# Gate and up tiles of four feed-forward blocks as a two by two product of quarters, with seven quarter products in place of eight

## What is computed

```python
def rms_norm(x, gain):
    xf = x.astype(jnp.float32)
    y = xf * lax.rsqrt(jnp.mean(xf * xf, axis=-1, keepdims=True) + NORM_EPS)
    return (y * gain.astype(jnp.float32)).astype(x.dtype)
...
def modulate(x, shift, scale):
    return x * (1 + scale) + shift
...
def swiglu(h, w_gu, w_down):
    gate, up = jnp.split(h @ w_gu, 2, axis=-1)
    return (jax.nn.silu(gate) * up) @ w_down
```

## Time and profile before

| | us |
|---|---|
| median of 3 runs | 3361.91 (3359.94 to 3364.61) |
| profiled execution | 3367.02, its span 3365.3 |
| PE busy (matmul) | 3231.2, 96% of the span |
| DVE busy | 1817.0, 54% |
| ACT busy | 1157.8, 34% |
| POOL busy | 439.7, 13% |

### The profile page before, as it was taken

One profiled execution on the slowest core, in us unless ns is written; L12 is line 12 of the kernel. 1 busy time (PEld: TensorE's weight loads), 2 busy tenths in 40 slices (PEclk: granted clock), 3 DMA queues, 4 the chain that ended last, 5 costly groups with the idle time before them and its releaser, 6 DMA issues. The chain is left out here.

```text
span 3365.3 us, 67083 instructions
## 1 busy us (share of the span) xinstructions
PE 3231.2 (96%) x28066; PEld 2765.1 (82%) x28066; DVE 1817.0 (54%) x2677; ACT 1157.8 (34%) x1839; POOL 439.7 (13%) x312
## 2 busy tenths in 40 slices
PE   6999999999988999999999999999999989899998
PEld 5888888886667878888888888888886668789897
DVE  4552554565667655543554553454555766655353
ACT  3331222225665333321222431222224654344231
POOL 2000001000705310000002000001100616120000
PEclk9999999999999999999999999999999999999999
DMA  5231221342000012222221222222232000122222
GB/s 201 91 109 66 94 96 60 127 156 89 1 17 3 4 57 81 93 98 77 90 90 57 94 98 71 81 93 85 85 141 110 2 18 3 34 88 94 90 91 94
DMA packets 68270, 263.34 MB, mean 78 GB/s; under 512 B 7552, under 2 KB 8704, under 8 KB 67456
## 3 DMA queue, kind: packets, MB, share of 16 engines
q1 hardware_dynamic: 67664, 256.95, 22.1%
q10 hardware_dynamic: 432, 3.88, 0.3%
HBM read 258.70 MB, written 2.10 MB: 77 GB/s over the span
## 5 line engine op out<-in xcount | busy, mean ns | idle before, releaser
L240 PE MATMUL ps<-hn_hi,w_hi 128*128 128x512 f32 (+1 forms) x3520 | 864.8, 327 | 17.9 <-DVE hn_lo L457 5.9
L240 PE MATMUL ps<-hn_hi,w_lo 128*128 128x512 f32 (+1 forms) x3520 | 865.4, 327 | 0.0
L240 PE MATMUL ps<-hn_lo,w_hi 128*128 128x512 f32 (+1 forms) x3520 | 861.1, 326 | 0.0
L217 ACT ACTIVATE w_hi<-raw 128x1024 fp32r<-128x1024 f32 (+1 forms) x300 | 338.5, 1128 | 1375.4 <-PE ps L240 1217.7
L222 DVE TENSOR_TENSOR w_lo<-raw,w_hi 128x1024 fp32r<-128x1024 f32 (+1 forms) x300 | 396.9, 1323 | 469.5 <-ACT w_hi L217 462.0
L240 PEld LDWEIGHTS ps<-hn_hi,w_hi 128*128 128x128 f32 x3520 | 547.9, 190 | 82.3 <-issue 17.6
L240 PEld LDWEIGHTS ps<-hn_lo,w_hi 128*128 128x128 f32 x3520 | 548.3, 190 | 58.3
L240 PEld LDWEIGHTS ps<-hn_hi,w_lo 128*128 128x128 f32 x3520 | 545.2, 190 | 58.1
L240 PE MATMUL ps<-g_hi,w_hi 128*128 128x512 f32 (+1 forms) x1424 | 398.0, 347 | 6.1 <-DVE g_lo L894 6.1
L240 PE MATMUL ps<-g_lo,w_hi 128*128 128x512 f32 (+1 forms) x1424 | 403.5, 351 | 0.0
L240 PE MATMUL ps<-g_hi,w_lo 128*128 128x512 f32 (+1 forms) x1424 | 397.5, 347 | 0.0
(11 more groups left out here) (274 smaller groups left out, 3795.8 us busy)
## 6 DMA issues: line engine op xcount, KB each, us to landing
raw<-wgu SPq DMA_DIRECT2D x176, 512.0 KB, 3.4
w_mod_one<-wmod SPq DMA_DIRECT2D x100, 512.0 KB, 3.3
raw<-wdn SPq DMA_DIRECT2D x64, 704.0 KB, 4.1
raw<-win SPq DMA_DIRECT2D x44, 512.0 KB, 4.5
w_mod_two<-wmod SPq DMA_DIRECT2D x28, 512.0 KB, 3.6
w_mod_first<-wmod_first SPq DMA_DIRECT2D x4, 2048.0 KB, 23.2
raw<-wout SPq DMA_DIRECT2D x16, 512.0 KB, 3.3
h<-xT ACTq DMA_DIRECT2D x1, 3072.0 KB, 9.8
```

The lines of the kernel that those rows point to most:

```text
L217: act.activation(w_hi[s][:, 0:kt, :].rearrange("p k n -> p (k n)"), raw[s][:, 0:kt * P], ACT.Copy).then_inc(hi_ready[s].sem, 1)
L240: mm = pe.matmul(out[:, o:o + b - a], w[:, k, :], m[:, k, a:b], start=(k == 0 and w is w_hi[s] and m is mov_hi), stop=(k == kt - 1 and w i ...
```

## The change

Gate and up tile of one pair, and the two halves of the tokens, are seen as a matrix product of 2x2 blocks: the weights are split in four quarters (gate and up, first four and last four k-tiles, each 4 k-tiles x 128 = 512 columns of `raw0` or `raw1`), the moving operand in four quarters (first and second half of the tokens, first and last four k-tiles, each 4 tiles of 384+2 columns, or 256+2 for 512 tokens). Eight quarter products would give the four result blocks; here seven do, over sums and differences of quarters. The seven moving operands are made once for a block (`m_hi0..6`, `m_lo0..6`), the weight sums (`slot_sum2..5`) for each pair by POOL, and the products are combined out of PSUM by DVE (`combine`, seven additions of 384 or 386 columns for each pair) after a first copy by ACT (`first_copy`).

Since sums over the two token halves need like factors, the tokens are normalised first: `x_norm` = `gained_h` * `rstd`, before any product of the block. The in-between stages before a block leave `gained_h` in one fp32 copy and no longer split it.

The down product is made after groups of 4, 2, 4, 4, 4 and 4 pairs (`DOWN_SIZES`) rather than after 11 and 11, so there are six down stages of 8 tiles in a block. The operand of the down product is a ring of four tiles. `raw` holds 1024 columns. The modulation rows (24, as before) are placed in the groups 0, 2 and 3 and the down stages that follow them. The loops of `ffn` are written out.

The core of the diff:

```diff
-        WS = NFH * P * 4
+        WS = KD * P * 4 + 1568
...
+        def gained_plain(act, tile, nt):
+            for span, w in tokens_of(nt):
+                mm = act.activation(gained_h[:, bass.ds(tile, 1), span].rearrange("p a t -> p (a t)"),
+                                    h[:, bass.ds(tile, 1), span].rearrange("p a t -> p (a t)"), ACT.Identity,
+                                    scale=moda[:, w, bass.ds(tile, 1)])
+            mm.then_inc(hn_hi_ready.sem, 1)
...
+                    for j, z in enumerate(SIZES):
+                        for n in range(FIRST[j], FIRST[j] + z):
+                            load_mods(n)
+                            gate_raw_free(n)
+                            load(0, A["wdn"][l, which, j, 0] if last_of(n) else A["wgu"][l, which, 2 * n + 2])
+                            up_raw_free(n)
...
+                    rstd_of = lambda half: rstd_s[:, half * HT:(half + 1) * HT].rearrange("p (a t) -> p a t", a=1).broadcast_to([P, LP, HT])
+                    pool.wait_ge(hn_hi_ready.sem, hn_hi_ready.at(KD + 1))
+                    for half in range(2):
+                        pool.wait_ge(rstd_ready.sem, rstd_ready.at(half + 1))
+                        pool.tensor_tensor(x_norm[:, half, LP:KD, 0:HT], gained_h[:, LP:KD, half * HT:(half + 1) * HT],
+                                           rstd_of(half), ALU.mult).then_inc(x_pool.sem, 1)
+                    slot_lo_made(pool, 4, 0)
+                    slot_lo_made(pool, 3, 0)
+                    moving_lo(3, lambda k: m_raw[3][:, k, 0:HW], 13, "T4b")
+                    slot_lo_made(pool, 6, 0)
...
+                    def next_pair(n, first):
+                        for p in (2, 3, 5) if first else (2, 3, 4, 5):
+                            weight_sum(pool, p, n)
+                        slot_lo_made(pool, 3, n)
+                        slot_lo_made(pool, 6, n)
+                        if first:
+                            weight_sum(pool, 4, n)
+                        slot_lo_made(pool, 4, n)
...
+            def weight_sum(eng, p, n):
+                a, b, op = {2: (quarter(2), quarter(3), ALU.add),
+                            3: (slot_sum[2][:, :], quarter(0), ALU.subtract),
+                            4: (quarter(0), quarter(2), ALU.subtract),
+                            5: (quarter(1), slot_sum[3][:, :], ALU.subtract)}[p]
...
+                eng.tensor_tensor(slot_sum[p][:, :], a, b, op).then_inc(w_summed.sem, 1)
...
+            def slot_lo_made(eng, p, n):
+                done = slot_lo_ready if (p, n) in lo_at else slot_lo_pool
+                eng.wait_ge(slot_hi_ready.sem, slot_hi_ready.at(hi_at[p, n]))
+                if p in (2, 3):
+                    eng.wait_ge(*sum_at(3 if p == 2 else 5, n))
+                src = quarter(3) if p == 6 else slot_sum[p][:, :]
+                eng.tensor_tensor(flat(slot_lo[p]), src, flat(slot_hi[p]).bitcast(F32), ALU.subtract).then_inc(done.sem, 1)
...
+                    def first_copy(n):
+                        act.wait_ge(*product_at(n, 0))
+                        if n:
+                            act.wait_ge(*combined_at(n - 1, 4))
+                        act.activation(base_s[:, 0:HW], bank(n, 0), ACT.Copy).then_inc(first_copied.sem, 1)
...
+                    def combine(n, p, out, x, *own):
+                        dve.wait_ge(*product_at(n, p))
+                        for k in own:
+                            dve.wait_ge(*combined_at(n, k))
+                        dve.tensor_tensor(out, x, bank(n, p)[:, 0:out.shape[1]], ALU.add).then_inc(combined.sem, 1)
+                    def gate_first(n):
+                        dve.wait_ge(first_copied.sem, first_copied.at(n + 1))
+                        combine(n, 1, gate_s[:, 0:HW], base_s[:, 0:HW])
+                    def with_sixth(n):
+                        combine(n, 3, base_s[:, 0:HW], base_s[:, 0:HW])
+                    def with_fifth(n):
+                        combine(n, 2, gate_s[:, C[1]], base_s[:, 0:HT], 2)
+                    def with_seventh(n):
+                        combine(n, 4, up_s[:, 0:HW], base_s[:, 0:HW], 2)
+                        combine(n, 4, up_s[:, C[1]], gate_s[:, C[1]], 3)
+                    def gate_second(n):
+                        combine(n, 5, gate_s[:, C[1]], gate_s[:, C[1]], 3)
+                    def up_first(n):
+                        combine(n, 6, up_s[:, 0:HW], up_s[:, 0:HW], 4)
+                    def silu(n, half):
+                        dve.wait_ge(tanh_ready.sem, tanh_ready.at(2 * n + half + 1))
+                        t = slice(half * HT, (half + 1) * HT)
+                        dve.scalar_tensor_tensor(out=tanh_s[:, t], in0=tanh_s[:, t], scalar=1.0, in1=gate_s[:, C[half]],
+                                                 op0=ALU.add, op1=ALU.mult).then_inc(silu_ready.sem, 1)
...
+                    def normed(k):
+                        dve.tensor_tensor(x_norm[:, 0, k, 0:HT], gained_h[:, k, 0:HT], rstd_s[:, 0:HT], ALU.mult).then_inc(x_own.sem, 1)
+                    normed(0)
+                    for k in range(LP):
+                        if k + 1 < LP:
+                            normed(k + 1)
...
+                            gate_first(n)
+                            if n and n == FIRST[j]:
+                                slot_lo_made(dve, 5, n)
+                            if not last_of(n):
+                                gate_lo_made(n + 1)
+                            elif z == 4:
+                                two_tiles_lo(j, "01")
+                            with_sixth(n)
+                            with_fifth(n)
+                            if not last_of(n):
+                                slot_lo_made(dve, 2, n + 1)
+                            elif z == 4:
+                                two_tiles_lo(j, "23")
+                            else:
+                                down_lo_made(dve, j, "01")
+                                down_lo_made(dve, j, "23")
+                            with_seventh(n)
+                            for m in mods_of.get(n, ()):
+                                mod_product(m)
+                            gate_second(n)
+                            up_first(n)
+                            silu(n, 0)
+                            glu_out(n, 0)
+                            silu(n, 1)
+                            glu_out(n, 1)
+                            if not last_of(n):
+                                slot_lo_made(dve, 5, n + 1)
+                            ring_lo_made(n, 0)
+                            ring_lo_made(n, 1)
...
+                    def gate_up(n):
+                        j, q = GROUP_OF[n], n - FIRST[GROUP_OF[n]]
+                        for o, p in enumerate(order_of(n)):
...
+                            for k in range(LP):
+                                if n == 0 and (p, k) in MOVING_AT:
+                                    x, v = MOVING_AT[p, k]
+                                    pe.wait_ge(x.sem, x.at(v))
+                                for w, m in ((slot_hi[p], M_OF[p][0]), (slot_hi[p], M_OF[p][1]), (slot_lo[p], M_OF[p][0])):
+                                    mm = pe.matmul(bank(n, p), w[:, k, :], m[:, k, 0:HW],
+                                                   start=(k == 0 and w is slot_hi[p] and m is M_OF[p][0]),
+                                                   stop=(k == LP - 1 and w is slot_lo[p]))
+                            mm.then_inc(product_done.sem, 1)
...
+                        together = 2 if z == 4 else 4
+                        for t in range(together):
+                            down(j, t, range(z - 1))
+                        for t in range(together):
+                            down(j, t, (z - 1,))
+                        for t in range(together, KD):
...
-                            if not (last and s == 1):
-                                gained_lo(dve, i * 2 + s, nxt[3], i * 2 + hn_hi_ready.at(s + 2))
...
+DOWN_SIZES = (4, 2, 4, 4, 4, 4)
```

712 lines of the change are left out of this document (542 added, 170 removed).

## The result

The changed kernel takes 3573.0 us (3560.6 to 3574.9, four runs) against 3363.3 for the kernel before in the same runs: 1.062 times as long, 95% interval 1.059 to 1.064. The forecast was 3568.

A forecast was written before the change was run, and what follows sets the result against it. PE's own pace was taken to bound the kernel before. Each 768 block: -45 +10 +23 +30 +21 = +39 us, three times +117; the fourth +89; in all 3361.9 + 206 = 3568 us, range 3390 to 3670.

The forecast's parts named there:

- PE's pace: In feed-forward blocks, PE's matmul spacing sets the time; matmuls of 386 columns would start 0.176 us apart.
- The term of -167: PE's gain from 84 matmuls for 96: 45 us in each of three blocks, 32 us in the fourth.
- One at a time on DVE and POOL: DVE instructions with two SBUF inputs and POOL instructions reading SBUF exclude each other; 13.5 us for a 768-token pair.
- Start: At a 768 block's start: chain +10 us, first pair 38 us (+23); for 512 tokens, +9 and +17.
- rival (4): Waits hold PE at 1.2 GHz through first pairs, squares come late in the last down stage: 3660 to 3700 us, chance 0.06.
- Pairs with a row: The 11 pairs with a modulation row in each 768 block need 15.6 to 18.6 us, taken as 17.5: +30 us.
- It does not pack without gaps: In pairs with a row, the load round of 11.7 us is held up by DVE instructions, some 4 to 6 us.
- Fourth block: At 512 tokens, load round and one-at-a-time work make pairs 13.5 us against PE's 10.2: +69, block sum +89 us.
- Down stages: Six per 768 block: three with modulation rows at +6 us each, three without at +1 each, together +21 us.
- (1): Rival: DVE and POOL pass each other freely; -34 us in all, 3328 us, chance 0.11.
- (2): Rival: all is covered and PE keeps its pace, with only the chain at four starts; 3227 us, chance 0.05.
- (3): Rival: DVE and POOL exclude each other but pack better; some 3475 us, chance 0.16.

The follow-up runs named there:

- e6: Kernel before, with unused POOL instructions added: additions in the first and fourth blocks, self-additions in the second, memsets in the third; 1.004 times the kernel before.
- e3: Changed kernel, with the squares of `h` in a block's last down stage made by ACT instead of POOL; 1.054 times the kernel before.
- e2: Changed kernel, with POOL's `x_norm` and `lo` parts at each block's start made by DVE; 1.049 times the kernel before.
- e9: Changed kernel, with the modulation row's product moved on DVE from ahead of `gate_second` to the pair's end; 1.093 times the kernel before.
- e12: Against e8, in pairs with a row: SP issues the row's load behind both weight loads, ACT makes `hi` of slots 5 and 6 earlier; 3349.3 us.
- e1: Changed kernel, with the four weight sums of each pair after a group's first moved from POOL to DVE; 1.078 times the kernel before.
- e5: Changed kernel, with ACT making `w_hi` of the next gate tile before the first half's tanh and biased copy; 1.046 times the kernel before.
- e8: Changed kernel with the edits of e2, e3 and e5 together, and the fourth block as in the kernel before; 3400 us.

## Why the prediction was right, and where it was not

**PE's pace.** 0.176 us forecast and measured. The term of -167 was too small by 23 us, for the most part because the pace of before was taken from stretches of 100 us and not from whole blocks. The down stages were forecast too low by 19 us, and the rest too high by 8: that 206 comes within 13 us of the 193.5 owes something to luck.

**One at a time on DVE and POOL.** Right, and shown by e6. With e3 and e2 it accounts for the dear last down stage and the dear start.

**Start.** The chain of 10 and the first pair of 38 came out at 10.4 and 36.0, for 512 tokens 9 and 27 at 7.9 and 26.4. PE's clock was taken to cost 0 to 3 us at a start. The low clock of rival (4) did come in the first pair of the second block, whose mean is 0.70: after its waits for operands, matmuls of 386 columns start 0.32 us apart, the level of 1.2 GHz, the last of them at 1359.7 us. But at 1363.9 PE stands once more for an operand, 1.1 us, so the low clock cost at most little; the pair behind it has 1.00. The rest of rival (4), 3660 us and more, did not come.

**Pairs with a row.** +30 against 27: right in size, wrong in reason, so the size is luck. Some 4 of the 27 are not the row's at all but the start's, since they go from the second pair in e2. For the others the step that failed is 15.6 us for the exclusive work of such a pair and then "It does not pack without gaps". The gaps were given to DVE's blocked instructions. The runs show a different thing: e9 has the same exclusive work and takes 20.0 us for a pair with a row in the second block, the changed kernel 17.4, e12 15.1. What filled the 2 to 5 us was SP, standing for the row's buffer with the gate tile's load behind it (in e9 with both), and ACT's `hi` of slot 6 behind a tanh that stood for the row; e12 shows the two together. The 15.6 itself was near: it is DVE's round of 15.46 in e12, of which PE sees little in a group of four pairs. The prediction named SP's round, but not that the row is the first in it.

**Fourth block.** 13.5 against 13.6 us for a pair. The step "With DVE's 3584 columns (3.8 us) and POOL's 8.9 us and gaps one at a time it is 13.2 at least" gives the number by a sum that does not bind: e1 lowers that sum and lengthens the pair, e5 leaves it and shortens the pair. In its place stand two rounds of nearly one length: DVE's queue (7.2 of work, about 4 blocked, 2.3 idle) and POOL's (about 11.5 with its own blocked time, and 2.1 idle for a load). Exclusion is in both, which would explain why the size came out; no run takes it away.

**Down stages.** +21 against 30.5, 17.6 and 25.1. The stages with rows were 4 to 6.5 us over, about as forecast. The last stage before an input projection was counted at +1 and cost 12: `hn_lo`, two inputs in SBUF, against POOL's squares. The sentence on it stood under rival (4) for the last, short stage; it belonged in the forecast.

**The rivals.** (1) and (2) have fallen by e6 and by pairs of 13.6 us. (3), better packing, is what e12 makes by hand: not a property of the engines, but of the order in four queues.

## What to carry to other kernels

Work moved off the busiest engine costs what the engines that feed it can carry, and two engines that exclude each other are one engine for that sum; count their work together before a change like this. Then read each queue in order, SP's too: a load that stands for a buffer holds all loads behind it, and two instructions moved in two queues gave back 46 to 50 us (e12 against e8), about as much as POOL's whole share of the start (e2). A sum that comes out at the right number is no proof of the mechanism: take away a part of the sum and see whether the time follows, as e1 did, or keep the sum and change the order, as e9 and e12 did.
